# Stick-breaking attention weights as a running product over the keys, turned on TensorE, with the values as three products of split operands

## The reference, cut to what matters

```
z = einsum('bhqd,bhnkd->bhqnk', q_blk, k_pre) * scale          # all keys before the query
log_1m = where(valid, log_sigmoid(-z), 0)                      # log(1 - sigmoid(z))
within = einsum('bhqnk,kj->bhqnj', log_1m, suffix)             # sum over later keys of the block
later = cumsum(totals, reverse) - totals                       # sum over later blocks
w = where(valid, exp(log_sigmoid(z) + within + later), 0)
o = einsum('bhqnk,bhnkd->bhqd', w, v_pre)
```

## Time and profile before

| | us |
|---|---|
| median of 3 runs | 2422.58 (2421.87 to 2423.89) |
| span of the profiled execution | 2420.3 |
| median less that span | 2.3 |
| TensorE busy | 2392.6 |
| VectorE / GpSimd / ScalarE busy | 1510.4 / 1252.9 / 1159.4 |

### The profile page before, as it was taken

The page is one execution under the profiler, slowest core; times in us unless marked ns, Lnnn a source line. Parts: engine busy times, 40 slices in busy tenths (PEclk is TensorE's granted clock), DMA queues, the critical chain, the costliest instruction groups (busy, mean ns, idle before and its releaser), DMA issues.

```text
span 2420.3 us, 30141 instructions
## 1 busy us (share of the span) xinstructions
PE 2392.6 (99%) x10448; PEld 1909.8 (79%) x10448; DVE 1510.4 (62%) x2002; ACT 1159.4 (48%) x1819; POOL 1252.9 (52%) x883
## 2 busy tenths in 40 slices
PE   8999999999999999999999999999999999999998
PEld 5877778888877888888777777678888777888887
DVE  6666752664496465468877777832764486466366
ACT  4566642343475245323577677842343474255230
POOL 1666653774365354444655555543864465444431
PEclk9999999999999999999999999999999999999999
DMA  5543322123213312372433333222123213322352
GB/s 205 170 127 123 95 96 100 45 87 122 92 57 118 126 62 87 99 280 92 134 102 104 91 126 102 72 92 92 53 79 131 89 52 117 126 74 74 121 184 78
DMA packets 130550, 258.66 MB, mean 107 GB/s; under 512 B 13024, under 2 KB 75488, under 8 KB 129376
## 3 DMA queue, kind: packets, MB, share of 16 engines
q1 hardware_dynamic: 128960, 252.02, 31.6%
q10 hardware_dynamic: 1440, 4.72, 0.6%
HBM read 197.97 MB, written 58.72 MB: 106 GB/s over the span
## 4 chain that ended last, share of the span: by engine, by line
PE 44%; DVE 2%; issue 2%; POOL 1%; ACT 1%; DMA 0%; POOLq 0%; SPq 0%; DVEq 0%; ACTq 0%
PE J L711 8%; PE J L712 8%; PE J L713 8%; PE Z L882 4%; PE OB L852 3%; PE OB L882 2%; PE ACC L882 2%; PE ACC L830 1%; PE ACC L832 1%; PE Z L712 1%; PE Z L713 1%; PE Z L711 1%; PE ACC L840 1%; PE ACC L842 1%; POOL PLO L2177 1%
## 5 line engine op out<-in xcount | busy, mean ns | idle before, releaser
L2131 POOL TENSOR_TENSOR WLS<-SR,WHS 128x512 fp32r<-128x512 f32 x264 | 411.0, 1575 | 150.4 <-ACT WHS L1037 143.5
L711 PE MATMUL J<-XBH,WHS 128*128 128x512 f32 x1152 | 451.8, 392 | 2.6 <-ACT ST L1110 2.0
L713 PE MATMUL J<-XBH,WLS 128*128 128x512 f32 x1152 | 448.7, 389 | 0.0
L712 PE MATMUL J<-XBL,WHS 128*128 128x512 f32 x1152 | 448.7, 389 | 0.0
L711 PE MATMUL J<-XBH,WH 128*128 128x512 f32 x864 | 345.5, 400 | 3.0 <-DVE XBL L1558 2.3
L713 PE MATMUL J<-XBH,WL 128*128 128x512 f32 x864 | 336.9, 390 | 0.0
L712 PE MATMUL J<-XBL,WH 128*128 128x512 f32 x864 | 336.7, 390 | 0.0
L2177 POOL TENSOR_TENSOR PLO<-PF,PHI 128x512 fp32r<-128x512 f32 (+3 forms) x160 | 194.6, 1216 | 140.3 <-DVE PHI L1750 139.1
L711 PEld LDWEIGHTS J<-XBH,WHS 128*128 128x128 f32 x1152 | 216.3, 188 | 51.6 <-ACT ST L1110 3.2
L713 PEld LDWEIGHTS J<-XBH,WLS 128*128 128x128 f32 x1152 | 216.2, 188 | 45.8
L1591 DVE TENSOR_TENSOR ST<-J,ST 128x512 f32<-128x512 f32 x160 | 109.8, 687 | 228.3 <-PE J L713 181.2
(11 more groups left out here) (342 smaller groups left out, 5045.7 us busy)
## 6 DMA issues: line engine op xcount, KB each, us to landing
RAW<-w SPq DMA_DIRECT2D x144, 512.0 KB, 3.7
pk_m<-MB SPq DMA_DIRECT2D x56, 512.0 KB, 5.2
MB<-pk_m SPq DMA_DIRECT2D x48, 512.0 KB, 4.1
KR<-pk_k SPq DMA_DIRECT2D x160, 128.0 KB, 2.2
BRAW<-w SPq DMA_DIRECT2D x64, 256.0 KB, 5.0
VR<-pk_v SPq DMA_DIRECT2D x160, 64.0 KB, 2.0
XRAW<-xt SPq DMA_DIRECT2D x8, 1024.0 KB, 13.2
OR<-w SPq DMA_DIRECT2D x16, 512.0 KB, 6.9
```

Of the source, the lines that this page charges most:

```text
L711: nc.tensor.matmul(to, wh, xh, start=first, stop=True, skip_group_check=True)
L712: nc.tensor.matmul(to, wh, xl, start=False, stop=True, skip_group_check=True)
L713: return nc.tensor.matmul(to, wl, xh, start=False, stop=True, skip_group_check=True)
L2131: low = G_.tensor_tensor(WLS[:, k, :], SR[:, k, :], WHS[:, k, :].bitcast(F32), ALU.subtract)
```

## The change

A step becomes a block j of 128 queries (partitions) by a chunk k of 512 keys (the free axis, reversed, so that the newest key comes first). There are as many steps of the same widths as before. Four of them (j = 0 to 3) make a group, with one chunk of queries and one chunk of keys; the groups go from the newest keys to the oldest. The weights are made by two sigmoids, a scan along the keys and one multiply; TensorE turns them block by block; two engines split them; and the values are made for the whole group in 12 products.

```diff
 def steps_of(half):
+        for k in range(own, -1, -1):
+            for j in range(BLOCKS):
+                out.append((c, k, j, C - P * (j + 1) if k == own else 0, k == own, k == 0))
-SUMS, USE = 3, 4
+TURN, TAIL = 2, 3
# halves_filled: SUMS -> TAIL
# tiles: three GR, three W, one WTH and WTL (high part and rest of the turned weights),
#        two KC (512 keys each), three VC (256 keys each); LEFT holds the carried product
+        ZB, TB_ = [Z0, Z1], [JX, ACC]
# TensorE
             def scores(half, h, s):
-                wait_if(pe, m_done, gs - 2)
+                if j == 0:
+                    pe.wait_ge(k_in[n % 2], 16 * (n // 2 + 1))
+                wait_if(pe, share_done, gs - 1)
+                pass3(ZB[gs % 2][:, a:C], (QH[:, q], QL[:, q]), (KC[n % 2][:, 0, a:C], KC[n % 2][:, 1, a:C]), True)
-            def sums(...)    # two products
-            def carry(...)   # two products
+            def turned(half, h, s):
+                pe.wait_ge(w_done, gs + 1)
+                wait_if(pe, wt_lo, gs - 1)
+                for b in range(j + 1 if diag else BLOCKS):
+                    mm = nc.tensor.transpose(TB_[gs % 2][:, b * P:(b + 1) * P], W[gs % NW][:, at_:at_ + P], IDENT[:])
+            def values(half, h, i):
+                pe.wait_ge(wt_lo, BLOCKS * (n + 1))
+                for b in range(BLOCKS):
+                    mm = pass3(OB[:, q:C], (v[:, 1 - b % 2, 0, :], v[:, 1 - b % 2, 1, :]),
+                               (WTH[:, b, q:C], WTL[:, b, q:C]), diag and b == 0)
             def attention(half, h):
+                for s in range(ns + TAIL + 1):
+                    if s < ns:
+                        scores(half, h, s)
+                    if TAIL <= s < ns + TAIL and (s - TAIL) % BLOCKS == BLOCKS - 1:
+                        values(half, h, (s - TAIL) // BLOCKS)
+                    if 0 <= s - TURN < ns:
+                        turned(half, h, s - TURN)
                     for k in range(halves_filled(half, h, s - 1), halves_filled(half, h, s)):
                         piece(*fill[k // 2], (k % 2,))
# ScalarE; Abs, Exp, Ln, Exp go, and both table loads of a head (one load a half stays)
+            def shares(half, h, s):
+                wait_if(act, left_done, gs - NW + 1)
+                nc.scalar.activation(GR[gs % NW][:, a:C], ZB[gs % 2][:, a:C], ACT.Sigmoid, scale=-1.0).then_inc(rest_done, 1)
+                wait_if(act, wt_done, gs - NW + 1)
+                nc.scalar.activation(W[gs % NW][:, a:C], ZB[gs % 2][:, a:C], ACT.Sigmoid).then_inc(share_done, 1)
+            def turned_hi(half, h, s):   # WTH <- TB_, after wt_done
+                # loop over s: shares(s), turned_hi(s - TURN), pieces
+            def values_hi(g, part):      # STL <- J, pieces 10 and 12 of a value pair
# VectorE; PF, ARG, PHI and the argument go
+            def masked(half, h, s):      # diagonal: z + NEVER, 128 x 128, before the sigmoids
+            def remainder(half, h, s):
+                dve.wait_ge(rest_done, gs + 1)
+                V_.tensor_tensor_scan(g, g, g, 1.0 if diag else LEFT[...], ALU.mult, ALU.min).then_inc(scan_done, 1)
+            def turned_lo(half, h, s):   # WTL <- TB_ - WTH, after wt_hi
+                # loop over s: remainder(s - 1), masked(s), turned_lo(s - TURN), pieces
+            # turned(g, part): waits v_hi and k_kept, subtracts instead of copying
# GpSimd; the rest PLO and the mask go
+            def weights(half, h, s):     # loop over s: weights(s - 1), pieces
+                pool.wait_ge(scan_done, gs + 1)
+                made = G_.tensor_tensor(w[:, a + 1:C], w[:, a + 1:C], r[:, a:C - 1], ALU.mult)
+                if not diag:
+                    made = G_.tensor_tensor(w[:, 0:1], w[:, 0:1], LEFT[:, (n - 1) % 2, j:j + 1], ALU.mult)
+                made.then_inc(w_done, 1)
+                G_.tensor_copy(LEFT[:, n % 2, j:j + 1], r[:, C - 1:C]).then_inc(left_done, 1)
# memory: keys in chunks of 512, values kept and loaded as high part and rest (twice the bytes);
# keys and values are written reversed ([:, ::-1]) by the pieces that take them out of PSUM
# room(g, 0) of a query pair waits for v_kept (both stores), before for k_kept
```

More of the change, by code:

```diff
@@ L90, in steps_of @@
     for c in range(NC):
-        q0 = (half * NC + c) * (C // P)
-        top = q0 + C // P - 1
-        for b in range(top, -1, -1):
-            out.append((c, b, P * max(b - q0, 0), b == top, b == 0, b >= q0))
+        own = half * NC + c
+        for k in range(own, -1, -1):
+            for j in range(BLOCKS):
+                out.append((c, k, j, C - P * (j + 1) if k == own else 0, k == own, k == 0))
     return out
@@ L100, with first_group @@
 ENDS = [[max(i for i, step in enumerate(s) if step[0] == c) for c in range(NC)] for s in STEPS]
-ND = NC * (C // P)
+ND = NC * BLOCKS
 def first_step(half, h):
     return half * HEADS * NS[0] + h * NS[half]
+def first_group(half, h):
+    return first_step(half, h) // BLOCKS
 def diagonals(half, h, s):
-    return (half * HEADS + h) * ND + sum(step[5] for step in STEPS[half][:s + 1])
+    return (half * HEADS + h) * ND + sum(step[4] for step in STEPS[half][:s + 1])
 def filling(half, h):
@@ L330, in build @@
         S_END = [first_step(half, HEADS) for half in range(HALVES)]
+        G_END = [first_group(half, HEADS) for half in range(HALVES)]
         def y_count(half, n, h=KB):
@@ L835, in carry @@
-            def carry(half, h, s):
-                gs = first_step(half, h) + s
-                c, b, a, first, end, diag = STEPS[half][s]
-                if not end:
-                    pe.wait_ge(arg_done, gs + 1)
-                    nc.tensor.matmul(ACC[:, a:C], CARRY[:], PHI[gs % 3][:, a:C], start=False, stop=False,
-                                     skip_group_check=True)
-                    nc.tensor.matmul(ACC[:, a:C], CARRY[:], PLO[gs % 3][:, a:C], start=False, stop=True,
-                                     skip_group_check=True)
@@ L1135, in piece @@
                     shared(g, 1, 0, 0, 6)
+                if g % PAIRS < 2 * HEADS and g % 2 and i in (10, 12):
+                    values_hi(g, 0 if i == 10 else 1)
+            def values_hi(g, part):
+                hh = g // PAIRS * HEADS + g % PAIRS // 2
+                act.wait_ge(v_tr, 2 * hh + part + 1)
+                nc.scalar.copy(STL[(hh + 2) % 3][:, part * C:(part + 1) * C], J[(g + 1) % 2][:]).then_inc(v_hi, 1)
             def split_keys(g):
@@ new lines, in masked @@
+                dve.wait_ge(z_done, gs + 1)
+                z = ZB[gs % 2][:, a:a + P]
+                V_.tensor_tensor(z, z, NEVER[:], ALU.add).then_inc(z_masked, 1)
+            def remainder(half, h, s):
+                gs = first_step(half, h) + s
+                c, k, j, a, diag, end = STEPS[half][s]
+                dve.wait_ge(rest_done, gs + 1)
+                if not diag:
+                    dve.wait_ge(left_done, gs - BLOCKS + 1)
+                g = GR[gs % NW][:, a:C]
+                V_.tensor_tensor_scan(g, g, g, 1.0 if diag else LEFT[:, (gs // BLOCKS - 1) % 2, j:j + 1], ALU.mult, ALU.min).then_inc(scan_done, 1)
@@ new lines, in turned_lo @@
+            def turned_lo(half, h, s):
+                gs = first_step(half, h) + s
+                c, k, j, a, diag, end = STEPS[half][s]
+                n, q = j + 1 if diag else BLOCKS, slice(j * P, (j + 1) * P)
+                dve.wait_ge(wt_hi, gs + 1)
+                wait_if(dve, pv_done, 2 * (gs // BLOCKS))
+                V_.tensor_tensor(WTL[:, 0:n, q], TB_[gs % 2][:, 0:n * P].rearrange("p (b q) -> p b q", q=P),
+                                 WTH[:, 0:n, q].bitcast(F32), ALU.subtract).then_inc(wt_lo, 1)
@@ L2183, in attention @@
                     piece(g, i)
-                for s in range(ns + USE):
+                for s in range(ns + TAIL + 1):
                     if 1 <= s <= ns:
-                        rest_p(half, h, s - 1)
+                        weights(half, h, s - 1)
                     if s:
```

304 lines of the change are left out of this document (122 added, 182 removed).

## The result

The kernel after takes **2498.23 us** (median of 4 runs, 2497.36 to 2499.22), the one before on the same chip 2422.81 (4 runs, 2421.87 to 2423.89). The ratio is 1.0313, 95% interval 1.0298 to 1.0327: 3.1% slower, where 2385 was forecast.

What follows compares the result with a forecast made beforehand. TensorE, busy 2392.6 of 2420.3 us, was taken as the bound. Removing 82.4 us of its work, less stalls of 17, 13.5 and 6.5 and 8 between heads, gained 37.4: 2422.6 to 2385, range 2348 to 2416.

Steps and rivals of the forecast that it cites:

- TensorE's products: TensorE's work per full 512-wide step falls 0.66 us to 1.82: 5.0 a half 0 head, 15.6 a half 1 head, 82.4 in all.
- The ring: Loop through four engines: transposes, ScalarE copy, VectorE subtraction, scan, GpSimd multiply and tiny product; 5.0 us for two steps.
- where it binds: Stalls only between a group's first and third transposes: 17 us in half 1 heads 0 to 2, 13.5 head 3, 6.5 half 0.
- T(0): T(s) means TensorE's transposes of step s, issued two steps after its scores; here a group's step 0.
- the two short turns: Loop turns without the 12 value products, three a group; two need 5.0 us of TensorE in half 1, heads 0 to 2.
- The overlap: VectorE's and GpSimd's pieces, GpSimd's being 0.9 us a step, mostly fit beside the loop; 0.7 us added for all engines.
- the 15.4 us that the prediction named as its refutation: Wrong if a full group of heads 0 to 2 takes under 13.0 or over 15.4 us; 13.7 expected in half 1.
- Filling: Other TensorE work in half 1, heads 0 to 2: one piece of six products, 1.38 us, each step.
- Rival 3, the clock: Idling in head 3 of half 1 puts half its 60 us of work at 1.2 GHz: 30 us more, 2415; chance 0.05.
- Rival 2: GpSimd's 1.58 us pieces stand before its multiplies, making the loop 8.2 us in heads 0 to 2: 2444; chance 0.09.
- Between heads: Value copy, subtraction and stores delay the next head's start: 1 us for each of 8 heads, 0 to 3 each, 8 us.
- Costed at nothing: Key and value loads a group ahead, reversed writes, the moved diagonal mask and SyncE's order add no separate time.

Runs made afterwards that it cites:

- (3): The change with its scan reading the scores' PSUM bank and a constant column, ScalarE writing the second sigmoid there in place: 2456.4 us, ratio 1.0141.
- 9: The change with values as one plain f32 product, no rest or subtraction: 2436.3 us; with multiply, tiny product and carry copy also on VectorE: 2418.0 us.
- 10: The change with plain f32 values and the scan from PSUM: 2415.2 us; also one step deeper: 2413.1; or with multiply, tiny product and carry copy on VectorE: 2429.4.

## Why the prediction was wrong

- **TensorE's products: right.** The forecast of 0.44 for four transposes is 0.41 (1345.97 to 1346.38), and products stay 0.23 apart at full clock. Added up from the trace, the products of a middle head of half 1 are 85 us against 102.2, 17 less for a forecast of 15.6.
- **The ring: its parts and its length were right, where it binds was not.** The two sigmoids "are off the ring", and the order of its parts holds. From T(0) to T(2) of a group, across the two short turns, it takes 5.9 us in the mean of heads 0 to 2 and 5.5 in head 3, for 5.7 and 5.3. That is luck in part: the tiny product ends 0.7 us behind the multiply for 0.10, and uses up what was kept for pieces. The step that failed is "Only between T(2) and T(0), across two short turns, is TensorE quick enough to wait". In a full group of heads 0 to 2, T(2) waits 1.3 us and T(3) 1.0 more (2.5 and 1.3 in head 3), and T(3) of a diagonal group 1.7 (2.5). That makes 17 us of such waits a head, and 26 in head 3, where the forecast had 5.75 and 13.5 with the values' waits in them. From T(1) to T(3) it is 6.7 us (7.2 in head 3): ScalarE's copy starts 0.4 to 0.5 us later than between T(0) and T(2), and in heads 0 to 2 the scan takes 1.77 us there. With the scan from PSUM the two ways are 5.1 and 5.9 us in heads 0 to 2.
- **The overlap: the other step that failed.** The scan was put at 1.5 us; it is 1.27 alone and 1.58 in the mean of heads 0 to 2, up to 2.32 in the trace. The tiny product was put at 0.10 and took 0.55. Against them, and against the pieces, stood "most of it fits beside, and I take 0.7 for all engines". Scan, multiply, tiny product and pieces can't lie beside each other on the two engines. I read 62% and 52% busy as two engines with room; for what holds the lock they are one, and it holds 92 of a head's 112.5 us. What this cost is known in part: with the scans alone out of it, 42 us come back (3). (A slip besides: the stalls of 0.7 and of 2.65 - 2.5 make 0.85 a group, not 0.95, some 1.5 us of the sum.)
- **Where it was lost.** Heads 0 to 2 of half 1: 114.2 - 87.2 = 27 a head against a forecast of 6 to 7; full groups of 13.2 to 18.6 us from scan to scan, 15.1 in the mean of four, for 13.7. Head 3: 109.9 - 65.3 = 45 against 14.5; full groups of 13.3 to 17.6 for 11.5. Half 0: 10.8 + 20 = 31 in all against 10.5. Only one of the four kinds of full group exceeds the 15.4 us that the prediction named as its refutation; the rest lies in the diagonal groups and at the turns of heads.
- **Filling** was put at one piece (1.38 us) a step; it is 48 half pieces over 31 passes of the loop, 1.07 us. TensorE had less to do in a short turn than I gave it, 0.6 us less in two, and T(2) had to wait that much more.
- **Rival 3, the clock, came true** besides, at 0.05 and priced at 30: it cost some 38 us, and not in head 3 alone (0.94 to 0.96 with heads 0 to 2, 0.83 with head 3). The one wait of 6.0 us at the start told nothing of waits in series. The Trainium skill (TensorE: Matmul & The Clock Gate, Part 1) has idling bring the clock down; here the trace agrees, with 0.83 where TensorE idles most and 1.00 before.
- **Rival 2**, GpSimd's pieces ahead of its multiplies, gave 2444 from long queues on GpSimd. No run moved GpSimd's pieces alone. With the multiply taken off GpSimd's queue the time went down by 18 us in 9, and up by 14 in 10. Its price was worked out with instructions at their own durations and is short by the lock.
- **Between heads** 8 us were taken. At the start of half 1 ScalarE waits 7.0 us for the store of the values, as the prediction argued for it, and TensorE 3.7 for ScalarE, more than the 3 that bounded a head. The turning of the value blocks waits 4.1 us in all for VectorE. The sum is near the forecast by luck: half of it is one head's, where 1 us was taken for each of eight.
- **Costed at nothing:** key and value loads stayed so (no such wait above 3 us in all). The diagonal mask on VectorE takes 0.28, as taken.
- The step that the prediction itself could have settled is the earlier trace rows: two modes, 2351 and 3065, were taken as the ends of a range. A look at what GpSimd did beside each gives the rule, and the durations alone then give an estimate like the 99 us a head above.

What stays open: how the loss divides between the lock and the order (42 us for the scans off the lock, 41 for the other order, 36 for one more step of distance, and they don't add), and what the multiplies and pieces in the lock cost. A third bank for the scores with the scan from PSUM was not tried.

## What to carry to other kernels

Before work is added to VectorE or GpSimd, sum as one engine every VectorE instruction with two SBUF inputs and every GpSimd instruction of the stage, each at its shortest duration; if that sum is near TensorE's time, the busy shares of the two are no sign of room. (It is an estimate from above: 99 us here, where the records cover 90 to 92.) Then lay out the ring with the longer of the two durations for what can meet the other engine, and look at the order on each engine too: here either remedy gave some 40 us. A PSUM operand takes a VectorE instruction out of that sum. When the same instruction shows two durations, look at what its neighbour engine did in each before calling the upper one noise, and price a wait of TensorE that recurs in each group at its length plus what the clock then costs.

## What the runs showed of the hardware

- A VectorE instruction with two SBUF inputs that is issued under a GpSimd instruction ends its own time less 0.13 to 0.2 us after it: 1.08 for a scan of 512 (1.27 alone), 0.55 for a 128x512 subtraction or multiply (0.68), 2.15 for a scan of 1024 (2.35). The start of the instruction is hidden in the wait.
- A scan of 128x512 takes 1.27 us, from SBUF as from PSUM, and a plain product of two such tiles 0.69.
- GpSimd takes 0.19 us for a 128x1 product and 1.27 for a 128x511 one.
- A VectorE subtraction with one operand in PSUM takes 0.69 us with or without GpSimd beside it.
- Added TensorE work in recurring waits made a kernel 14 us faster, at a mean clock of 0.994 for 0.983.
